# A two-layer decoder trunk with a mixture of experts on one core: rows of each lot fetched by indirect DMA, weighted results sent to memory and read back per token, last norm on token rows

## What is computed

```python
def moe_swiglu(h, router, w1, w3, w2):
    logits = (h @ router).astype(F32)
    topv, topi = lax.top_k(logits, TOP_K)          # TOP_K = 2 of N_EXPERTS = 8
    wts = jax.nn.softmax(topv, axis=-1)
    gates = jnp.sum(jax.nn.one_hot(topi, N_EXPERTS, dtype=F32) * wts[..., None], axis=-2)
    out = jnp.zeros(h.shape[:-1] + (D_MODEL,), F32)
    for e in range(N_EXPERTS):
        out = out + gates[..., e:e + 1] * swiglu(h, w1[e], w3[e], w2[e]).astype(F32)
    return out
...
        x = (x.astype(F32) + gt2 * fo).astype(dt)  # gt2: one gate row for the prompt, one for each sample
...
    y_prompt = rmsnorm(xp, final_g).astype(x_prompt.dtype)
    y_sample = rmsnorm(xs, final_g).astype(x_sample.dtype)
```

## Time and profile before

| | |
|---|---|
| median of three runs | 1486.15 us |
| lowest and highest of them | 1478.11 and 1492.23 us |
| span of the profiled execution | 1480.3 us |
| PE, DVE, ACT, POOL busy in it | 1443.5, 1081.0, 836.0, 7.8 us |
| lots | 8 |

### The profile page before, as it was taken

One profiled execution on the slowest core, in us unless ns is written; L12 is line 12 of the kernel. 1 busy time (PEld: TensorE's weight loads), 2 busy tenths in 40 slices (PEclk: granted clock), 3 DMA queues, 4 the chain that ended last, 5 costly groups with the idle time before them and its releaser, 6 DMA issues.

```text
span 1480.3 us, 21800 instructions
## 1 busy us (share of the span) xinstructions
PE 1443.5 (98%) x8271; PEld 1217.0 (82%) x8271; DVE 1081.0 (73%) x1454; ACT 836.0 (56%) x873; POOL 7.8 (1%) x28
## 2 busy tenths in 40 slices
PE   8999999999999999999999999999999999999997
PEld 4888878999988888777788888888888888888886
DVE  3488424554544874269989998999899888988995
ACT  3344433444333435247676677777776777777765
POOL 1000000000000000000000000000000000000000
PEclk8899999999999999999999999999999999999997
DMA  9986686954559722448799899799898997997970
GB/s 302 313 274 209 207 258 195 283 182 161 182 177 334 257 86 93 158 179 325 278 327 393 297 367 389 272 394 369 296 393 302 360 393 270 393 391 273 394 277 30
DMA packets 259016, 408.38 MB, mean 276 GB/s; under 512 B 9880, under 2 KB 151904, under 8 KB 258944
## 3 DMA queue, kind: packets, MB, share of 16 engines
q1 hardware_dynamic: 243712, 397.22, 76.1%
q10 hardware_dynamic: 15232, 10.18, 2.3%
HBM read 401.49 MB, written 5.95 MB: 275 GB/s over the span
## 4 chain that ended last, share of the span: by engine, by line
PE 88%; DVE 8%; ACT 3%; issue 1%; ACTq 0%; DVEq 0%
PE ps L806 20%; PE ps L808 20%; PE ps L807 20%; PE ps L693 7%; PE ps L794 4%; PE ps L577 2%; DVE slab_lo L1817 2%; PE ps L645 2%; PE ps L953 1%; PE ps L898 1%; DVE uT L1564 1%; PE ps L672 1%; PE ps L531 1%; PE ps L768 1%; PE ps L760 1%
## 5 line engine op out<-in xcount | busy, mean ns | idle before, releaser
L1817 DVE TENSOR_TENSOR slab_lo<-ring,slab_hi 128x2048 fp32r<-128x2048 f32 x264 | 602.5, 2288 | 55.8 <-ACT slab_hi L1352 55.4
L1352 ACT CAST slab_hi<-ring 128x2048 fp32r<-128x2048 f32 x261 | 497.9, 1908 | 147.1 <-PE ps L808 146.3
L806 PE MATMUL ps<-slab_hi,tokens_hi 128*128 128x512 f32 (+1 forms) x768 | 289.9, 378 | 3.1 <-issue 1.7
L807 PE MATMUL ps<-slab_lo,tokens_hi 128*128 128x512 f32 (+1 forms) x768 | 286.6, 373 | 0.0
L808 PE MATMUL ps<-slab_hi,tokens_lo 128*128 128x512 f32 (+1 forms) x768 | 286.6, 373 | 0.0
L806 PEld LDWEIGHTS ps<-slab_hi,tokens_hi 128*128 128x128 f32 x768 | 144.2, 188 | 32.3 <-DVE slab_lo L1817 5.4
L808 PEld LDWEIGHTS ps<-slab_hi,tokens_lo 128*128 128x128 f32 x768 | 144.2, 188 | 26.6
L807 PEld LDWEIGHTS ps<-slab_lo,tokens_hi 128*128 128x128 f32 x768 | 144.3, 188 | 24.1
L693 PE MATMUL ps<-hT,ring 128*128 128x264 f32 x704 | 160.9, 387 | 0.0
L693 PEld LDWEIGHTS ps<-hT,ring 128*128 128x128 f32 x704 | 132.3, 190 | 22.3 <-issue 0.8
L1765 DVE TENSOR_TENSOR slab_lo<-ring,slab_hi 128x2048 fp32r<-128x2048 f32 (+1 forms) x34 | 75.8, 2229 | 96.9 <-ACT slab_hi L1283 96.9
(11 more groups left out here) (373 smaller groups left out, 1938.8 us busy)
## 6 DMA issues: line engine op xcount, KB each, us to landing
ring<-in_moe_w SPq DMA_DIRECT2D x264, 1024.0 KB, 9.5
ring<-in_mod_w SPq DMA_DIRECT2D x48, 1024.0 KB, 8.5
ring<-in_ffn_w SPq DMA_DIRECT2D x30, 1024.0 KB, 5.8
ring<-in_w_in SPq DMA_DIRECT2D x24, 1024.0 KB, 10.0
ring<-in_w_out SPq DMA_DIRECT2D x8, 1024.0 KB, 6.4
out_new_S_sample<-S ACTq DMA_DIRECT2D x8, 512.0 KB, 3.0
ring<-in_ffn_w SPq DMA_DIRECT2D x4, 768.0 KB, 4.2
uT<-in_x_prompt SPq DMA_DIRECT2D x1, 1024.0 KB
```

The source lines that it names most:

```text
L806: mm(out, x, w, start=start, stop=False)
L807: mm(out, x, wl, start=False, stop=False)
L1352: cp(wH[t % 3][:, :], w).then_inc(s_hi, 1)
L1817: tt(wL[t % 3][:, :], w, wH[t % 3][:, :].bitcast(fp32), ALU.subtract).then_inc(s_lo, 1)
```

## The change

**Rows in.** Lot 0 picks its rows as before. PE or ACT pick none for the later lots. POOL adds high and low rows together and stores all 264 token rows in memory (`rows_hbm`). DVE and PE make a table of which token and which weight stands in each slot of each lot (`table`, `lot_table`, in lot 0). For every later lot POOL issues one indirect DMA that fetches the 128 rows (`pick_rows`), as soon as PE has turned the lot before's. PE turns them as before.

**Rows out.** `outputs` on ACT weights the slots and writes them as plain rows. ACT stores them in memory (`y_hbm`, 512 KB a lot, at t = 5 of the next lot). `scatter`, `acc` and the turned gates are gone. `y_hbm` is first filled with zeros by one DMA of ACT ahead of the mixture (thirteen times 512 KB). In the last lot POOL fetches, for 128 prompt tokens, the next 128 and the 8 samples in turn, the two rows of each token that lots 0 to 6 wrote (`yback`, two buffers), and DVE adds the pair, multiplies by the gate row and adds to the residual (`combine`, at t = 14 to 22).

**Residual in rows.** The residual is needed as token rows. In lot 0 PE turns it and the gate columns back by 32 transposes in eight groups (`turn_rows_of`, at t = 11, 13, ..., 25), and ACT copies each group out at the next t (`rows_out`). Gate rows go to memory and come back spread over the partitions.

**The end.** The last lot's result is weighted and gated by DVE, split by ACT and DVE, and placed on tokens by twelve PE products of 512 columns. The last norm works on rows: squares with a running sum on ACT, the factors, and the scaling with the final gain on DVE, POOL and ACT.

The diff, cut to its core:

```diff
+            pool.wait_ge(s_gth, 2)
+            for t in range(2):
+                g.tensor_tensor(out=h2raw[:, t, :], in0=h2H[:, t, :].bitcast(fp32), in1=h2La[:, t, :].bitcast(fp32),
+                                op=ALU.add)
+            pool.wait_ge(s_tbl, 1)
+            ch(g.tensor_tensor(out=h2raw[0:NS, 2, :], in0=h2H[0:NS, 2, :].bitcast(fp32), in1=yrows[0:NS, :],
+                               op=ALU.add))
...
+            def pick_rows(n, tokens):
+
+                pool.wait_ge(s_pkT, 2 * n)
+                g.tensor_copy(pick_at, tokens).then_inc(s_pka, 1)
+                pool.wait_ge(s_pka, n)
+                pause()
+                pool.indirect_dma_start(picked[:, :], None, rows_hbm[:, :],
+                                        bass.IndirectOffsetOnAxis(pick_at, 0)).then_inc(s_pkd, 16)
...
+            pool.wait_ge(s_yst, final_lot * 16 + 16)
+            pause()
+            for t in range(3):
+                if t:
+                    pool.wait_ge(s_cmb, t)
+                for j in range(2):
+                    k = 2 * t + j
+                    pool.indirect_dma_start(yback[j][0:ROWS[t], :], None, y_hbm[:, :],
+                                            bass.IndirectOffsetOnAxis(back_idx[0:ROWS[t], k:k + 1], 0))\
+                        .then_inc(s_ybk, 16)
...
+            def turn_rows_of(n):
+
+                pe.wait_ge(s_xtr, n)
+                t, q = divmod(n, 2)
+                for c in range(4):
+                    if t < 3:
+                        last = nc.tensor.transpose(ps[7][0:ROWS[t], c * P:(c + 1) * P],
+                                                   xT[:, 4 * q + c, t * P:t * P + ROWS[t]], ident[:])
...
-                    if t in SCATTER_AT:
-                        c = SCATTER_AT[t]
-                        pe.wait_ge(s_gT, i + 1)
-                        pe.wait_ge(s_yl, i * 2 + 1 + c // 4)
-                        pe.wait_ge(s_scd, i * KC + c + 1)
-                        scatter(ps[7], c)
-                    if t == GATES_AT:
-                        pe.wait_ge(s_scd, i * KC + KC + 1)
-                        pe.wait_ge(s_gat, i + 1)
-                        turn_gates()
-                    if t == LAST_SLAB[0, NB - 1] and not final:
-                        pe.wait_ge(s_sel, i + 2)
-                        pe.wait_ge(s_mua, i * NB + NB - 1)
-                        gather(0)
-                        gather(1)
+                    if first and t == TABLE_TURN:
+                        lot_table()
+                    if first and t in ROWS_AT:
+                        if ROWS_AT[t] == 0:
+                            pe.wait_ge(s_tbl, 3)
+                        turn_rows_of(ROWS_AT[t])
...
+                    act_.dma_start(y_hbm.rearrange("(n p) d -> p n d", p=P),
+                                   xr[:, 0, :].unsqueeze(1).broadcast_to([P, MAXLOTS + 1, D])).then_inc(s_yst, 16)
...
+            def store_outputs(n, constant):
+
+                act_.wait_ge(s_yt, n * 2)
+                dst = y_hbm[(n - 1) * LOT:n * LOT, :] if constant else y_hbm[bass.ds((n - 1) * LOT, LOT), :]
+                act_.dma_start(dst, yrows[:, :]).then_inc(s_yst, 16)
+
+            def rows_out(n):
+
+                act_.wait_ge(s_xtp, n + 2)
+                t, q = divmod(n, 2)
+                dst = (xr[:, 0], xr[:, 1], x8[0:NS], gate_p[0:COND])[t]
+                A(dst[:, q * 512:(q + 1) * 512], ps[7][0:dst.shape[0], :], ACT.Copy).then_inc(s_xtr, 1)
...
                     cp(wH[t % 3][:, :], w).then_inc(s_hi, 1)
-                    if t == 3:
-                        outputs(i)
+                    if t == 3 and not first:
+                        outputs(i, constant)
+                    if t == 5 and not first:
+                        store_outputs(i, constant)
+                    if first and t - 1 in ROWS_AT:
...
+                        rows_out(ROWS_AT[t - 1])
...
+            def combine(step):
+
+                t, part = divmod(step, 3)
+                n = ROWS[t]
+                back, rows = yback[0][0:n, :], (xr[:, 0], xr[:, 1], x8[0:NS])[t]
+                if part == 0:
+                    dve.wait_ge(s_ybk, 32 * (t + 1))
+                    ch(tt(back, back, yback[1][0:n, :], ALU.add))
+                elif part == 1:
+                    ch(tt(back, back, (gate_s[0:NS, :] if t == 2 else gate_p[:, :]), ALU.mult))
+                else:
+                    tt(rows, rows, back, ALU.add).then_inc(s_cmb, 1)
...
-FOLD_AT = {25 + c: c for c in range(KC)}
-SCATTER_AT = {5 + 2 * c: c for c in range(KC)}
-ADD_AT = {t + 3: c for t, c in SCATTER_AT.items()}
-CHOOSE_AT = {25 + k: k for k in range(4)}
-REST_AT = {8 + 2 * k: k for k in range(2 + MAXLOTS - NE)}
-GATES_AT = 22
+TABLE_AT = {3: 0, 5: 1, 9: 2, 11: 3, 13: 4, 15: 5, 17: 6, 19: 7}
+TABLE_TURN = 7
+ROWS_AT = {11 + 2 * n: n for n in range(8)}
+COMBINE_AT = {14 + k: k for k in range(9)}
+PLACE_AT = 24
+FINAL_BANK = ((0, 1), (2, 3), (6, 7))
```

More of the change, by code:

```diff
@@ L517, in _ @@
+            for q in range(2):
+                qs = slice(q * 512, (q + 1) * 512)
+                pool.wait_ge(s_sq, KC * 2 * L + 3 * q + 2)
+                g.tensor_tensor(out=xr[:, 1, qs], in0=xr[:, 1, qs], in1=fg_row[:, qs], op=ALU.mult).then_inc(s_xg, 1)
         @block.tensor
@@ L906, in turn_picked, with lot_table, lot_products @@
                 last.then_inc(s_pkT, 1)
[L908 to L919, removed]
+            def lot_table():
+                pe.wait_ge(s_tbl, 2)
+                for n, (t, j) in enumerate((t, j) for t in range(3) for j in range(2)):
+                    last = mm(ps[7][:, 0:2 * MAXLOTS], slot_hit[0:ROWS[t], j, t, :], lot_hit[0:ROWS[t], t, j, :],
+                              start=(n == 0), stop=(n == 5))
+                last.then_inc(s_xtp, 1)
+            def turn_rows_of(n):
[6 more added lines that the diff above has]
+                    else:
+                        last = nc.tensor.transpose(ps[7][0:COND, c * P:(c + 1) * P],
+                                                   modT[:, 1, 5 * KC + 4 * q + c, :], ident[:])
+                last.then_inc(s_xtp, 1)
+            def lot_products(i, first=False, final=False):
                 for t, (kind, b, h) in enumerate(LOT_ORDER):
@@ L935, in lot_products @@
                         g = 2 * b + h
-                        if g == 0:
-                            pe.wait_ge(s_yl, i * 2 + 2)
+                        if g == 0 and not first:
+                            pe.wait_ge(s_yt, i * 2)
                         if h == 0:
@@ L983, in moe @@
                 gather(1)
-                turn_picked(0, 0)
-                turn_picked(0, 1)
-                lot_products(0)
+                for q in range(2):
+                    pe.wait_ge(s_pk, q + 1)
+                    turn_picked(0, q)
+                lot_products(0, first=True)
                 pe.wait_ge(s_tab, 1)
@@ L1360, in lot_act @@
                         A(sg[:, 0:WIDE[b]], ps[b % 2][:, 0:WIDE[b]], ACT.Silu).then_inc(s_mus, 1)
-                    if t == LS - 3 and not final:
-                        pick(i + 1)
                     if t == LS - 2 and not final:
@@ new lines, in final_square @@
+            def final_square(q, t):
+                act_.wait_ge(s_x, 3 * q + t + 1)
+                rows = (xr[:, 0], xr[:, 1], x8[0:NS])[t]
+                A((yback[0], yback[1], picked)[t][0:ROWS[t], q * 512:(q + 1) * 512], rows[:, q * 512:(q + 1) * 512], ACT.Square,
+                  accum_out=sq_part[0:ROWS[t], 2 * t + q:2 * t + q + 1]).then_inc(s_sq, 1)
+            for t in range(3):
+                final_square(0, t)
+            for t in range(3):
+                final_square(1, t)
+                r = rs_row[0:ROWS[t], t:t + 1]
+                act_.wait_ge(s_feb, t + 1)
+                act_.wait_ge(s_sq, KC * 2 * L + 4 + t)
+                ch(A(r, sq_part[0:ROWS[t], 2 * t + 1:2 * t + 2], ACT.Ln, scale=1.0 / D, bias=sq_eps[0:ROWS[t], t:t + 1]))
+                A(r, r, ACT.Exp, scale=-0.5).then_inc(s_rs, 1)
@@ L1924, in lot_dve @@
                     split_lot_slab(i, t)
-                    if first and t in REST_AT:
-                        rest_of_routing(REST_AT[t])
+                    if first and t in TABLE_AT:
+                        table(TABLE_AT[t])
                     if t in FORM_AT:
```

331 lines of the change are left out of this document (198 added, 133 removed).

## The result

The changed kernel takes 1500.83 us (median of four executions, 1499.58 to 1504.14), the kernel before 1487.42 (1478.11 to 1492.23). The ratio is 1.0097, with an interval of 1.0058 to 1.0137: about 1% slower, outside the range of the prediction. The profiled execution has a span of 1498.2 us against 1480.3.

A forecast was written before the change was run, and what follows sets the result against it. PE was taken to bound the kernel. Terms -29 + 19.5 + 10 - 6.3 = -5.8 against the profiled 1480.3 gave 1474.5; with the runs' median 5.85 above the span, the forecast was 1480 us, range 1460 to 1498.

The forecast's parts named there:

- What bounds the kernel: Lots 1 to 6: PE sets the pace at 99.6 us a lot, with DVE at 90 and DMA at 87.
- Middle lots, -29: Lots 1 to 6: PE loses scatters, turned gates and the gather, 4.8 us a lot, with no new limit.
- Rival 2: SP's queue, lots 1 to 7: extra rows make DMA the bound, kernel at 1509 us; chance 0.12.
- Lot 0, +19.5: Lot 0: saved work -0.6, eight PE stalls of 2.2 us behind rows_out +17.6, table and POOL +2.5.
- the +1.9 of the sum: Lot 0 apart from the readers: PE's net work -0.6 plus table and POOL together +2.5.
- POOL beside DVE: Lot 0: POOL's three additions hold up DVE; 1 us of PE loss taken, about 3 by the skill's rule.
- Last lot, +10: Final lot: saved work -2.5, combine steps +6.3, waits for second and third gather pairs +4.5 and +1.8.
- The combine steps in a row: Final lot, t = 14 to 22: nine DVE steps of 1.2 us make PE stand still 6.3 us.
- The end, -6.3: After the last product: 22 us become 15.5 through the new weighting, placing and norm; bounds -3 and -8.
- Ahead of the mixture, 0: Before lot 0: the 6.8 MB zero fill is hidden and costs 0; without the cover up to 17 us.
- Rival 1: Lot 0 and final lot: the stalls do not come, 1463 us, or 1456 with gathers hidden too; chance 0.2.
- Rival 3: The forecast itself: PE's saving real, latency stalls in lot 0 and the final lot, 1470 to 1494; chance 0.68.

The follow-up runs named there:

- experiment 1: Changed kernel with each rows_out copy on ACT one slab later (t - 2 instead of t - 1): 1466.78 us, ratio to the kernel before 0.9886.
- experiment 9: Changed kernel with later rows_out, own buffers for second gathers, half zero fill, combine every second slab, ACT copies replacing POOL's additions: 1444.15 us, ratio to before 0.9733.
- experiment 4: Changed kernel without POOL's three additions, storing only the high parts of the rows: 1496.75 us, ratio to the kernel before 1.0074.
- experiments 2 and 3: Each against the changed kernel: 2, second pair of final-lot gathers into own buffers, 1480.81 us; 3, zero fill cut from 13 blocks to 6, 1498.09 us.
- experiments 4 and 5: Each against the changed kernel: 4, no POOL additions, 1496.75 us; 5, the last four of eight rows_out one slab later, 1482.05 us.

## Why the prediction was wrong

**What bounds the kernel.** Right. PE sets the pace, and each stretch is explained by what PE does or waits for.

**Middle lots, -29.** Right in cause, and low by 3.6: 99.62 - 94.19 = 5.4 us a lot instead of 4.8. No new limit was met. DVE's busy time fell by 7.4 us a lot (90.2 to 82.9), where near 10 was forecast. The DMA engines now run at 382 to 384 GB/s over a whole lot and still keep PE fed: 94.2 us of PE work with no wait. A slab's landing went from 9.5 us to 13.1, and no engine waited for it. Rival 2 is refuted.

**Lot 0, +19.5, measured +34.3.** This is the step that failed most. The chain was right (reader, cast, low part, PE), and so was the number of stalls. Their size was 2.4 us with the clock up instead of 2.2, worth 2 us in all. The term that was missing is what a standstill does to PE afterwards: 12.5 us. The prediction took the time of a slab after a stall to be 2.75 us, a value read in a kernel that never stood still, and no term for the clock stands anywhere in its sum or bounds (-6, +3). All of lot 0 apart from the readers is +2.25 (experiment 1), near the +1.9 of the sum, but by luck, for two errors cancel. POOL's additions cost 4.0 and not 1. All the rest, table and saved work, was to be +0.9, and without the additions lot 0 is 93.81 us (experiment 9), 2.1 less than before. Half of that is PE's waiting, 2.2 us there and 3.2 before.

**POOL beside DVE.** The sentence on the Trainium skill, page SBUF — State Buffer, section Who interferes with whom, gave PE about 3 us by its rule where I gave 1. The trace agrees with the rule: a DVE operation of 0.16 us took 2.38 beside the third addition, the low parts beside the first two 3.28 and 3.01 instead of 2.29, and experiment 4 measures 4.0 us for the three.

**Last lot, +10, measured +18.4.** The two waits of DVE for gathers were predicted as 4.5 and 1.8 and measure 8.28 and 6.76; without them the lot is 15.3 us shorter, which takes in the clock lost behind them. The row that was taken for the landing was that of a plain DMA; what was left out is POOL's own time to issue, some 4 us a pair, and that eight rows are little faster than 128 (9.0 against 11.1 us, with less on the DMA engines). The combine steps in a row were oversized, 2.8 us instead of 6.3. The Trainium skill, page DMA: Bandwidth & Descriptors, section Anatomy of one DMA, gave 4.4 us for the pair: the measurement is 11.1 us from release to use, 5.7 to 8.8 for one DMA from issue to landing, and it decides.

**The end, -6.3, measured -6.15.** Right, step by step from the last product: weighting begins 0.44 us behind its start, ACT's high part 1.28 behind it, as the sum had them.

```profile
1482.15 0.40 PE L904 MATMUL ps<-slab_hi,act_lo 128*128 128x512 f32 x1
1482.59 1.41 DVE L2104 SCALAR_TENSOR_TENSOR y_gated<-ps,lot_tables,gate_rows_slots 128x512 f32<-128x512 f32 x2 [3.34 <-PE ps L904]
1483.43 1.23 ACT L1496 CAST y_hi<-y_gated 128x512 fp32r<-128x512 f32 x2 [4.69 <-DVE y_gated L2104]
```

**Ahead of the mixture, 0.** The fill is hidden, as said. The +3.9 us of the profiled execution belong to a spread that the prediction had only in the runs' median.

**The rivals.** Rival 1 (no stalls) is refuted by the waits and by experiment 1. Rival 3, the forecast, had the mechanism and a little over half its price. The last lot's stalls, 15.3 + 2.8 = 18.1 us, lie inside the prediction's own bounds of 6 to 20; lot 0's +34.3 lies far above its 13.5 to 22.5. Those bounds were drawn from waits alone, so they could not hold a second effect of the same waits.

## What to carry to other kernels

Price a stall of PE twice: the wait, and the slower products behind it. In this kernel a repeated wait of 2.4 us cost 4.0. Where work has to be read off PE by an engine that also feeds PE, put the reader one stage later than the one that makes it; that one number was worth over 2% here. When a DMA comes from POOL and its buffer is freed by the very engine that wants the data, count the release, the issue and the landing as one chain (9 to 11 us here, even for eight rows), or give it a buffer of its own.

## What the runs showed of the hardware

- Adding 64 products that nobody reads to PE's waits took about 16 us off the kernel's median; in the profiled executions lot 0 went from 130.2 us at a granted clock of 0.88 to 117.6 at 0.99.
- The same pattern of waits left the clock at 1.00 for five pairs of slabs in two profiled executions (experiments 2 and 3), and the clock fell in the first or second pair in three others (the kernel after, experiments 4 and 5). In the kernel after it stayed at 0.78 to 0.86, in windows of 12 us, until the pattern ended.
- One indirect DMA occupied POOL for 0.86 to 2.84 us in the kernel after, and those that fetched rows for lots 2 to 7, with the DMA engines at a share of 1.03, landed 6.1 to 6.4 us after issue.
- Beside a POOL addition of 2.39 us a DVE multiplication of three columns took 2.38 us instead of 0.16. Two POOL additions of 1024 columns took 8.70 us together beside DVE's low parts, which grew by 1.0 and 0.7 us; one of 512 columns at the end, with no low part beside it, took 1.26.
